# GLA level blocks copied by ScalarE in rectangles, and a gate order with another lag

## What is computed

```python
def _gla_chunk_scan(q, k, v, log_a, state0):
    ...
    diff = cum[:, :, :, None, :] - cum[:, :, None, :, :]
    decay = jnp.exp(jnp.where(mask, diff, -jnp.inf))
    att = jnp.einsum('bhid,bhjd,bhijd->bhij', qf, kf, decay)
    o = o_inter + jnp.einsum('bhij,bhje->bhie', att, vf)

def _conv_module(u, p):
    a, g = jnp.split(u, 2, axis=-1)
    h = a * jax.nn.sigmoid(g)
    h = _depthwise_conv(h, p['conv_dw'], p['conv_db'])
    h = jax.nn.silu(_layer_norm(h, p['conv_ln_g'], p['conv_ln_b']))
    return h @ p['conv_wo']
```

## Time and profile before

| | us |
|---|---|
| median of 3 runs | 3352.45 |
| lowest and highest | 3349.76, 3353.37 |
| the profiled execution | 3348.97 |
| span of that execution, first to last instruction | 3347.1 |
| PE busy | 3078.4 |
| DVE busy | 1744.8 |
| ACT busy | 1143.3 |
| mean granted clock of PE | 0.959 |

### The profile page before, as it was taken

One profiled execution on the slowest core, in us unless ns is written; L12 is line 12 of the kernel. 1 busy time (PEld: TensorE's weight loads), 2 busy tenths in 40 slices (PEclk: granted clock), 3 DMA queues, 4 the chain that ended last, 5 costly groups with the idle time before them and its releaser, 6 DMA issues.

```text
span 3347.1 us, 40311 instructions
## 1 busy us (share of the span) xinstructions
PE 3078.4 (92%) x16299; PEld 2270.8 (68%) x16299; DVE 1744.8 (52%) x2837; ACT 1143.3 (34%) x1831; POOL 382.1 (11%) x190
## 2 busy tenths in 40 slices
PE   7988799999998979999898889998999899898998
PEld 3665554444444468844587665788988898897897
DVE  3258977451221368821538774228863444545554
ACT  4023220032231143301623113328655344434443
POOL 2000000000000024400000000000011243330342
PEclk7999899999999999999898999999999999998999
DMA  6222213422323213222322232245552465332562
GB/s 202 79 72 76 88 63 126 126 79 88 112 89 126 82 58 99 93 69 59 95 63 75 77 108 84 89 137 166 174 182 77 130 185 163 128 120 73 151 177 88
DMA packets 419323, 362.34 MB, mean 108 GB/s; under 512 B 20229, under 2 KB 392550, under 8 KB 419140
## 3 DMA queue, kind: packets, MB, share of 16 engines
q1 hardware_dynamic: 416928, 359.11, 34.8%
q10 hardware_dynamic: 1028, 0.39, 0.0%
q0 software_dynamic: 1184, 0.28, 0.0%
HBM read 358.70 MB, written 1.05 MB: 107 GB/s over the span
## 4 chain that ended last, share of the span: by engine, by line
PE 71%; DVE 17%; issue 5%; ACT 5%; DMA 2%; POOL 0%; SPq 0%; POOLq 0%; DVEq 0%; ACTq 0%
PE banks L1041 13%; PE banks L871 8%; PE banks L820 7%; DVE conv_out L2457 6%; PE banks L903 5%; PE banks L905 5%; PE banks L904 5%; PE banks L1023 5%; PE banks L894 3%; DVE gla_att L2519 1%; ACT narrow_hi L1540 1%; PE banks L1072 1%; PE banks L1238 1%; PE banks L1288 1%; PE banks L1221 1%
## 5 line engine op out<-in xcount | busy, mean ns | idle before, releaser
L903 PE MATMUL banks<-operand_narrow,narrow_hi 128*128 128x256 f32 x1312 | 393.4, 300 | 48.8 <-DVE operand_narrow L2740 23.6
L790 POOL TENSOR_TENSOR narrow_lo<-wring,narrow_hi 128x1024 fp32r<-128x1024 f32 x100 | 250.4, 2507 | 1498.6 <-ACT narrow_hi L1540 1498.6
L2258 DVE TENSOR_TENSOR narrow_lo<-wring,narrow_hi 128x1024 fp32r<-128x1024 f32 (+2 forms) x180 | 239.8, 1335 | 307.6 <-ACT narrow_hi L1540 307.3
L904 PE MATMUL banks<-operand_narrow,narrow_hi 128*128 128x256 f32 x1312 | 377.3, 288 | 0.0
L905 PE MATMUL banks<-operand_narrow,narrow_lo 128*128 128x256 f32 x1312 | 377.1, 287 | 0.0
L1540 ACT ACTIVATE narrow_hi<-wring 128x1024 fp32r<-128x1024 f32 (+2 forms) x280 | 283.9, 1022 | 149.5 <-PE banks L905 142.3
L903 PEld LDWEIGHTS banks<-operand_narrow,narrow_hi 128*128 128x128 f32 x1312 | 257.9, 197 | 59.8 <-issue 37.5
L2457 DVE SCALAR_TENSOR_TENSOR conv_out<-conv_in,vectors,conv_out 128x512 f32<-128x512 f32 (+1 forms) x464 | 286.6, 618 | 15.3
L1041 PE MATMUL banks<-operand_a,wring 128*128 128x512 f32 (+1 forms) x768 | 258.3, 491 | 7.1 <-DMA wring<-in_w_in_dram 4.2
L904 PEld LDWEIGHTS banks<-operand_narrow,narrow_hi 128*128 128x128 f32 x1312 | 258.1, 197 | 1.7
L905 PEld LDWEIGHTS banks<-operand_narrow,narrow_lo 128*128 128x128 f32 x1312 | 257.8, 196 | 0.0
(11 more groups left out here) (355 smaller groups left out, 5755.3 us busy)
## 6 DMA issues: line engine op xcount, KB each, us to landing
wring<-in_w_in_dram SPq DMA_DIRECT2D x52, 1024.0 KB, 5.3
wring<-in_w_ada_dram SPq DMA_DIRECT2D x48, 1024.0 KB, 5.5
wring<-in_ffn_wup_dram SPq DMA_DIRECT2D x44, 1024.0 KB, 5.1
wring<-in_w_ff_in_dram SPq DMA_DIRECT2D x32, 1024.0 KB, 5.4
wring<-in_w_ff_out_dram SPq DMA_DIRECT2D x32, 1024.0 KB, 5.6
wring<-in_ffn_wdown_dram SPq DMA_DIRECT2D x32, 704.0 KB, 4.4
wring<-in_w_in_dram SPq DMA_DIRECT2D x36, 512.0 KB, 5.2
wring<-in_w_in_dil_dram SPq DMA_DIRECT2D x18, 1024.0 KB, 5.0
```

The source lines that it names most:

```text
L790: pool.tensor_tensor(NL[:, v % 4, 0:kn, :], w, NH[:, v % 4, 0:kn, :].bitcast(F32), ALU.subtract).then_inc(ev("narrow_lo_pool"), 1)
L903: pe.matmul(out, wh, a[:, 0:SEQ], start=first, stop=False)
L904: pe.matmul(out, wh, a[:, SEQ:512], start=False, stop=False)
L2258: tt(NL[:, v % 4, 0:kn, :], w, NH[:, v % 4, 0:kn, :].bitcast(F32), ALU.subtract).then_inc(ev("narrow_lo"), 1)
```

## The change

1. `pick` on DVE leaves out the levels 64 and 32 as well (steps i = 2 to 5); it starts at level 16.
2. ACT's new `rectangles(l, c0, i)` does those levels, called at its steps 3 to 6 for i = 2 to 5, after the exp of that step and before what is due. For each b and each group of 2s rows it copies one rectangle (s keys by 4 heads by s queries), with no mask: for s = 64 one rectangle a tile, 64 x 256, for s = 32 two, 32 x 128. The last one of a tile frees its bank.
3. `due` and `due_late` take a `gate_lag`, by default 2, which counts in layer 1 only. DVE calls them with 3; ACT calls them as before.

```diff
@@ -673,15 +673,15 @@
-    def due(l, n):
+    def due(l, n, gate_lag=2):
 
         def items(step, what):
             return [item for item in window[l][step] if item[0] == what] if 0 <= step < len(window[l]) else []
-        return items(n - 2, "ada") + items(n - (2 if l else 3), "g")
-
-    def due_late(l):
-
-        return [item for n in range(3) for item in due(l, len(window[l]) + n)]
+        return items(n - 2, "ada") + items(n - (gate_lag if l else 3), "g")
+
+    def due_late(l, gate_lag=2):
+
+        return [item for n in range(3) for item in due(l, len(window[l]) + n, gate_lag)]
@@ -1762,6 +1762,21 @@
+            def rectangles(l, c0, i):
+
+                s, d = STEPS[i]
+                for b in range(2):
+                    t = F[f"ga{l}.{c0}.{i}"] + b
+                    act.wait_ge(*done(t))
+                    if i == 2:
+                        act.wait_ge(*freed(F[f"ga{l}.{c0}.qk"] + b))
+                    src = bank(t).rearrange("p (h i) -> p h i", h=4)
+                    for g in range(0, P, 2 * s):
+                        queries, keys = (slice(g + h.start, g + h.stop) for h in halves(d, s))
+                        ins = act.activation(AT[keys, b, :, b * P + queries.start:b * P + queries.stop],
+                                             src[keys, :, queries], ACT.Copy)
+                    ins.then_inc(*free(t))
@@ -1787,6 +1802,8 @@
+                if 3 <= i <= 6:
+                    rectangles(l, c0, i - 1)
                 if i == 15 and c0 == 0:
@@ -2505,15 +2522,12 @@
                 s, d = STEPS[i]
-                if s == P:
+                if s >= 32:
                     return
                 for b in range(2):
                     t = F[f"ga{l}.{c0}.{i}"] + b
                     dve.wait_ge(*done(t))
-                    if i == 2:
-                        dve.wait_ge(*freed(F[f"ga{l}.{c0}.qk"] + b))
-                    else:
-                        dve.wait_ge(*freed(F[f"ga{l}.{c0}.{i - 1}"] + b))
+                    dve.wait_ge(*freed(F[f"ga{l}.{c0}.{i - 1}"] + b))
@@ -2554,7 +2568,7 @@
-                for what, *of in due(l, n_step):
+                for what, *of in due(l, n_step, 3):
@@ -2566,7 +2580,7 @@
-            for what, *of in due_late(l):
+            for what, *of in due_late(l, 3):
```

## The result

The changed kernel takes 3323.51 us (median of 5 runs, 3317.64 to 3324.73) against 3352.45 us of the kernel before, measured beside it; the ratio is 0.9912 with a 95% interval of 0.9898 to 0.9925, so the gain is about 29 us where 22.5 was forecast. Its profiled execution took 3318.62 us with a span of 3316.8 us, at a mean granted clock of 0.964 (before: 3347.1 us and 0.959).

The account below looks back on a forecast made before the run. The prediction took DVE to bound both GLA stages (conv_out taps, then masked copies). Layer 0's 5.2 us plus layer 1's 17.3 made 22.5, so 3352.45 - 22.5 = 3330.0 us, chance 0.70; range 3323 to 3340.

Parts of the forecast that it names:

- Step (a): Layer 1: first taps come a step later, six taps (3.1 us) move to the output phase; no gain or loss by 1975 us.
- The output matmuls of layer 1: Layer 1's GLA output matmuls: start about 25 us earlier than 1849.5 (5.2 plus 20.4); no gain of their own forecast.
- Layer 1's loop: Layer 1's GLA steps: pairs 4.92, five vanished waits 14.6, new wait -2.6, conv_in behind the loop +0.4; 17.3 us gain.
- the new wait: Start of layer 1, diff 7: DVE, now faster, waits 2.6 us for PE's GLA tile.
- Layer 0: GLA stage of layer 0: masked copies saved on DVE less rectangles delaying the gate, 5.2 us gain over both sets.
- Set 2: Layer 0, second 16 steps: all four pairs count, 4.92 us, less 1.1 at the gate.
- Set 1: Layer 0, first 16 steps: pairs of steps 4 and 5 give 0, steps 6 and 7 2.46 us, less 1.1 at the gate.
- Rival B: Layer 0: dearer rectangles at the gates and PE eat the whole gain; 3335 us, chance 0.11.
- Rival C: Layer 1: the five vanished waits become waits for PE; half of 14.6 lost, 3337 us, all lost 3344.6; chance 0.10.
- Rival D: Layer 1 loop: new pauses hold PE at 1.2 GHz, losing 49 us; slower, 3379 us, chance 0.04.
- (c): Layer 1 loop: conv_in frees its bank later, so PE stands about 2.8 us every second step; hidden, with little cover.
- Rival E: Behind the GLA stages: a wait that does not move swallows the gain; 3350 us, chance 0.05.

Follow-up runs that it names:

- debt_early: The changed kernel with six more conv_out taps paid at the end of layer 1's GLA loop, ahead of the r merges: 3326.10 us, ratio 0.9921.
- rect_only: The kernel before with only the rectangles moved to ACT, gate order as before on both engines: 3339.04 us, ratio 0.997.
- lag_only: The kernel before with only DVE's later conv_in in layer 1, all masked copies staying on DVE: 3333.88 us, ratio 0.9948.

## Why the prediction was right or wrong

The sign and the main cause were right. The size was not: 22.5 us were forecast, 26.0 lie in the touched stages, and the median of 3323.51 stands at the low end of the range (the ratio makes it 3322.9, just under it). The 26.0 are 22.5 + 3.1 + 1.7 - 1.3, by the three steps below.

**Step (a), the six taps (mis-sized, 3.1 us).** "... six taps (3.1 us) run in the output phase instead, where DVE is still the bound: neither gain nor loss by 1975 us." The sum had no term for it. DVE had 5.5 us of idle time behind the last merge, a wait for ACT that the profile of before shows, and the merge had 3.7 us of slack; debt_early shows that the taps fit in there: "r, wo" is 0.0 with them there and +3.2 with them ahead. The 69.8% of the earlier trace rows said that DVE bounds the phase; it did not say that DVE bounds its end. The sum of gains should have had +3.1 for it, where it had nothing (1.4 of it were lost again behind, in MLA, by a change of PE's clock that no term had either).

**The output matmuls of layer 1 (no term, 1.7 us).** The forecast put the start of the outputs at 20.4 us of loop gain and the loop gave 20.5. But the first two groups of output matmuls then ran at 2.4 GHz (granted clock 1.00 from 1819.5 us) instead of 1.2 (0.51 from 1849.4 to 1852.9 us in the kernel before). Of before is the earlier trace rows (1849.48, 2.03 us for four) and

```profile
1851.30 1.83 PE L1196 MATMUL banks<-gla_e,gla_state 128*128 128x256 f32 x4
```

and the changed kernel has

```profile
1820.52 1.10 PE L1192 MATMUL banks<-gla_att,gla_v 128*128 128x256 f32 x4 [1.25 <-DVE gla_att L2533]
1821.46 1.03 PE L1196 MATMUL banks<-gla_e,gla_state 128*128 128x256 f32 x4
```

(2.03 - 1.10) + (1.83 - 1.03) = 1.7 us, and the "out" column has it in every kernel with the new order and in none without it. PE had waited 2.36 us before the first of them, now 1.25.

**Layer 1's loop (right).** Pairs 4.92, waits 14.6, the new wait of 2.74 (forecast 2.6), `conv_in` 0.4 and the taps that left: 4.92 + 14.6 - 2.74 + 0.4 + 3.1 = 20.3, measured 20.5. rect_only and lag_only show the two parts singly. So layer 1 came to 17.3 + 3.1 + 1.7 = 22.1 us; the table has 22.2.

**Layer 0 (right in kind, 1.3 us too high).** Set 2 was forecast at 3.8 and gave 3.4. Set 1 was forecast at 1.4 and gave 0.5: the pairs of steps 4 and 5 gained nothing and the gate lost 1.1, both as said; that set 1 ends on PE, and that PE's conv tile there would take 8.18 us instead of 7.66, was not seen. The other 0.4 us of set 1 and the 0.4 of set 2 stay open.

**Rival B (layer 0 gives nothing)** falls with 3.8 us in layer 0 and copies of 268 ns. **Rival C (the waits turn into waits for PE)** falls too: inside the loop DVE has no wait for PE behind 1745.32. **Rival D (the clock)** had the sign wrong. PE's granted clock in the loop, before and after:

```profile
1741.00:1849.40 108.40, 91.25 (x479) 81.68 (x477) 87.65 (x160) 35.77 (x37) 0.00 (x0) 0.87 0.27 70
```

```profile
1732.50:1819.50 87.00, 81.78 (x479) 73.70 (x477) 78.46 (x144) 39.12 (x49) 0.00 (x0) 0.98 0.32 85
```

The pause at the bank of `conv_in` did come, as (c) said: three waits, 4.9 us in all, the longest 2.6 (the `PE banks L1288` row above; I had taken 2.8 for every second step). But PE's four waits for DVE in the old loop are gone:

```profile
PE banks L1172 <- DVE gla_e_more L2502: 7.9, 2, 4.6
PE banks L1172 <- DVE gla_e L2502: 6.9, 2, 3.6
```

14.8 us of pauses up to 4.6 us became 4.9 us of pauses up to 2.6, and the clock rose from 0.87 to 0.98. These long pauses of PE were the other end of DVE's waits for the sigmoid: rect_only, which keeps those waits, keeps 15.3 us of such pauses (granted clock 0.91 from 1741 to 1850 us), and lag_only has 0.3 us of them left beside 6.8 of the new kind (0.97). I counted the new pause without the four that went. The Trainium skill's page "TensorE: Matmul & The Clock Gate" (Why this matters for your kernels) wants no long gaps between bursts of matmuls; I had cited it against the change, and by these rows it speaks for it. **Rival E** falls: the gain reaches the end but for 0.3 to 0.5 us in "rest". That is a net figure: 1.3 us are lost in MLA (above) by the first profile, and 1.8 come back between 3290 and 3311 us; why, was not tested.

**The chances.** The range was too narrow below: it allowed 3323 for copies at nothing and a wait that goes, but no bound for a term that had been set to zero by an argument, and none for what moves from one execution to the next in code that is not touched (a single profile of the same kernel lay 7 us apart, the medians of before between 3347.84 and 3353.15).

## What to carry to other kernels

A debt that is moved to "where the engine is still the bound" can be free if the engine has a wait at the end of that phase: read the last wait before the phase's end, not the phase's share, and leave out of it what the engine itself starts with its last piece of work in the phase. When an engine waits for a result that a third engine queues behind other work, ask for the result one step later (or start it one step earlier) before making the work cheaper: here 14.6 and 13.4 us came from order, 7 (by the stages of rect_only) from work moved off DVE. And a pause that a change adds to TensorE must be weighed with the pauses that it takes away: here fewer and shorter ones went with a clock of 0.98 instead of 0.87.

## What the hardware showed that was not expected

ACT's copy out of a bank goes by columns and not by partitions down to small sizes: 266 ns for 2 x 128, 268 for 32 x 128, 368 for 64 x 256. Four of 32 x 128 in a row take 1.12 us, so they pace at 0.28 and do not overlap; two of 64 x 256 take 0.62 to 0.65 us, so the second starts 0.26 to 0.28 after the first and they do overlap, by 0.10. The Trainium skill's page "ScalarE: Activation LUTs" (What ACT_TABLE_LOAD costs) gives 186 ns + 0.833 ns per element, which is 293 and 399 ns, and an overlap of 93 ns between neighbours; the single copies are 25 to 31 ns shorter here, the pairs of 64 x 256 agree with the overlap, and the pace of 0.28 of the 32 x 128 ones against its 0.20 does not.

The copies between two exps needed no table load: at 222.06 they follow the exp directly, and the load comes only ahead of the sigmoid, at 224.33.

The same kernel, unchanged, showed a granted clock of 1.00 in one execution and 0.81 in another, in the same 20 us of MLA, with PE busy throughout in both, and was 4.4 us later behind it. A loss of this kind in one profile, 3.5 to 6.7 us over "between" here, must not be put down to an edit; the touched stages repeated to 0.2 us.
